# One loop for turns 1 to 9 of the experts, with the overflow part and the residual rows moved ahead of it

## The reference, cut to what matters

```python
for e in range(N_EXPERTS):                       # 32 experts, EXPERT_FF = 512
    h = jax.nn.silu(t @ w_gate[e]) * (t @ w_up[e])
    out = out + combine[:, e:e + 1] * (h @ w_down[e])
```

## Time and profile before

| | |
|---|---|
| three executions | 1076.65, 1077.33, 1078.59 us, median 1077.33 |
| profiled execution | span 1076.0 us, first to last instruction; its time outside the span isn't listed, the median is 1.3 us more |
| busy share of the span | PE 76%, PEld 61%, DVE 29%, ACT 18%, POOL 1% |
| read from memory | 437.84 MB, 408 GB/s over the span |
| chain that ended last | DMA 53%, PE 40%, issue 4%, DVE 2% |
| mean granted TensorE clock | 0.892 |

### The profile page before, as it was taken

The page is one execution under the profiler, slowest core; times in us unless marked ns, Lnnn a source line. Parts: engine busy times, 40 slices in busy tenths (PEclk is TensorE's granted clock), DMA queues, the critical chain, the costliest instruction groups (busy, mean ns, idle before and its releaser), DMA issues.

```text
span 1076.0 us, 30244 instructions
## 1 busy us (share of the span) xinstructions
PE 820.6 (76%) x13956; PEld 653.4 (61%) x13957; DVE 315.3 (29%) x782; ACT 192.6 (18%) x360; POOL 5.4 (1%) x26
## 2 busy tenths in 40 slices
PE   9999989673767667666899999896556767666685
PEld 9778757452654545555599977664354545555463
DVE  5764522211111111111277744221101111111112
ACT  6764211000000000000254331010000000000002
POOL 1000000000000000000000000000000000000000
PEclk9999999987887888888999999998879888888889
DMA  9987999999999999999998599999999999999995
GB/s 375 427 332 282 422 427 427 429 441 425 433 427 434 433 432 431 433 433 421 418 428 336 219 396 424 426 427 429 444 425 428 432 432 433 429 435 433 433 420 242
DMA packets 24948, 439.94 MB, mean 409 GB/s; under 512 B 2992, under 2 KB 3504, under 8 KB 8240
## 3 DMA queue, kind: packets, MB, share of 16 engines
q1 hardware_dynamic: 23904, 437.58, 95.9%
q10 hardware_dynamic: 976, 1.33, 0.4%
HBM read 437.84 MB, written 1.05 MB: 408 GB/s over the span
## 4 chain that ended last, share of the span: by engine, by line
DMA 53%; PE 40%; issue 4%; DVE 2%; SPq 1%; ACT 1%; DVEq 0%; ACTq 0%
DMA ring<-in_expert_weights 50%; PE psum L1579 12%; PE psum L1375 6%; PE psum L1588 6%; PE psum L1448 4%; PE psum L1596 3%; PE psum L1608 3%; PE psum L1427 2%; DMA ring<-in_even_w_in 2%; DMA m<-in_gmlp_w_s 1%; PE psum L1602 1%; PE psum L1700 1%; DVE ring_halves L875 0%; PE psum L1347 0%; PE psum L1334 0%
## 5 line engine op out<-in xcount | busy, mean ns | idle before, releaser
L1579 PE MATMUL psum<-ring,m 128*32 128x128 f32 x7936 | 304.1, 322 | 221.5 <-DMA ring<-in_expert_weights 187.2
L1579 PEld LDWEIGHTS psum<-ring,m 128*32 128x32 f32 x7936 | 280.7, 132 | 252.5 <-issue 177.9
L1236 DVE TENSOR_TENSOR m<-psum,m 128x128 f32<-128x128 f32 x64 | 18.7, 292 | 549.3 <-ACT m L769 532.4
L1588 PE MATMUL psum<-ring,m 128*32 128x256 f32 x1984 | 123.3, 387 | 5.2 <-DMA ring<-in_expert_weights 3.9
L769 ACT ACTIVATE m<-psum 128x128 f32<-128x128 f32 x60 | 16.7, 278 | 497.1 <-PE psum L1579 497.1
L1375 PE MATMUL psum<-scr_halves,ring_halves 128*128 128x256 f32 x736 | 99.1, 284 | 0.2 <-ACT ring_halves L603 0.2
L1588 PEld LDWEIGHTS psum<-ring,m 128*32 128x32 f32 x1984 | 66.1, 113 | 52.9 <-issue 12.1
L1375 PEld LDWEIGHTS psum<-scr_halves,ring_halves 128*128 128x128 f32 x736 | 94.3, 193 | 0.5 <-ACT ring_halves L603 0.5
L1596 PE MATMUL psum<-m 32*128 32x256 f32 x1024 | 81.1, 420 | 10.6 <-issue 8.5
L1608 PE MATMUL psum<-x,m 128*32 128x256 f32 x1024 | 72.7, 402 | 1.4 <-issue 0.8
L1596 PEld LDWEIGHTS psum<-m 32*128 32x128 f32 x1024 | 50.2, 195 | 29.6 <-issue 23.6
(11 more groups left out here) (196 smaller groups left out, 522.5 us busy)
## 6 DMA issues: line engine op xcount, KB each, us to landing
ring<-in_expert_weights SPq DMA_DIRECT2D x36, 6144.0 KB, 33.7
ring<-in_expert_weights SPq DMA_DIRECT2D x76, 2048.0 KB, 21.9
ring<-in_odd_w_in SPq DMA_DIRECT2D x5, 2048.0 KB, 26.0
ring<-in_even_w_in SPq DMA_DIRECT2D x3, 2048.0 KB, 22.2
ring<-in_even_w_out SPq DMA_DIRECT2D x2, 2048.0 KB, 31.4
spare<-in_expert_weights SPq DMA_DIRECT2D x2, 2048.0 KB, 24.7
ring<-in_last_down SPq DMA_DIRECT2D x8, 512.0 KB, 32.1
ring<-in_odd_w_out SPq DMA_DIRECT2D x2, 2048.0 KB, 28.9
```

Source lines behind the costliest of these rows:

```text
L1579: last = pe.matmul(GU[CAP * part:CAP * (part + 1), lo:lo + FP], block_of(k), w_of(k)[:, FP * part:FP * (part + 1)], start=k == 0, stop=k = ...
L1588: last = pe.matmul(YB[CAP * part:CAP * (part + 1), 0:DP], h[:, CAP * f:CAP * (f + 1)], w[:, f, DP * part:DP * (part + 1)], start=f == 0, s ...
```

## The change

- TensorE, ScalarE, VectorE: turn 0 is written out, then come the residual rows (TensorE) and the overflow part, then one loop over turns 1 to 9. `PAUSE`, the expert after which the overflow part stands, goes from 14 to 2.
- SyncE: `overflow` comes after experts 4 and 5 have been issued and ahead of expert 6. The transfers themselves, their sizes and what they wait for stay.
- A whole expert's DMA now counts on `landed` of its gate slot; two `sem_inc` on SyncE raise those of its up and down slots at the issue. TensorE waits for gate's first, so it doesn't use the others early. All later experts use the same three waits.

```diff
-MIDDLE = 5
-PAUSE = MIDDLE * TRI - 1
+PAUSE = TRI - 1
...
+def landed_count(n):
+    return sum(z <= n and place(z) == place(n) for z in COUNTED)
...
-                sp.dma_start(ring[:, SLOT * 3 * at:SLOT * 3 * (at + 1)], expert_weights_in[l, e]).then_inc(whole_landed[at], 16)
+                sp.dma_start(ring[:, SLOT * 3 * at:SLOT * 3 * (at + 1)], expert_weights_in[l, e]).then_inc(landed[3 * at], 16)
+
+                sp.sem_inc(landed[3 * at + 1], 16)
+                sp.sem_inc(landed[3 * at + 2], 16)
...
-                for e in range(EARLY + 2, FINE):
+                for e in range(EARLY + 2, 2 * TRI):
+                    second(l, e)
+                overflow(l)
+                for e in range(2 * TRI, FINE):
                     second(l, e)
...
-                turns(l, ROLLED + 1, MIDDLE + 1)
-                overflow(l)
-                turns(l, MIDDLE + 1, TURNS)
+                turns(l, ROLLED + 1, TURNS)
...
-                for start, stop in ((0, MIDDLE), (MIDDLE, TURNS)):
-                    with act.Fori(start, stop) as b:
-                        for i in range(TRI):
-                            expert(l, b * TRI + i)
-                    if start == 0:
-                        more_experts(l)
+                for e in range(TRI):
+                    expert(l, e)
+                more_experts(l)
+                with act.Fori(1, TURNS) as b:
+                    for i in range(TRI):
+                        expert(l, b * TRI + i)
...
-                for start, stop in ((1, MIDDLE), (MIDDLE, TURNS)):
-                    with dve.Fori(start, stop) as b:
-                        for i in range(TRI):
-                            expert(l, b, i)
-                    if start == 1:
-                        more_experts(l)
+                more_experts(l)
+                with dve.Fori(1, TURNS) as b:
+                    for i in range(TRI):
+                        expert(l, b, i)
...
-            def whole_expert(l, T, i):
-                n = entry(l, FINE + i)
-
-                def wait_weights(mat):
-                    if mat == 0:
-                        pe.wait_ge(whole_landed[place(n) // 3], (T + (whole_count(l, FINE + i) - ROLLED)) * 16)
+                    pe.wait_ge(landed[place(n + mat)], (T + (landed_count(n + mat) - 1)) * 16)
...
-                with pe.Fori(1, ROLLED) as T:
-                    for i in range(TRI):
-                        apart_expert(l, T, i)
-                with pe.Fori(ROLLED, MIDDLE) as T:
-                    for i in range(TRI):
-                        whole_expert(l, T, i)
                 for t in range(TT):
                     put_x(t)
                 more_experts(l)
-                with pe.Fori(MIDDLE, TURNS) as T:
+                with pe.Fori(1, TURNS) as T:
                     for i in range(TRI):
-                        whole_expert(l, T, i)
+                        later_expert(l, T, i)
```

More of the change, by code:

```diff
@@ L76, in third @@
     return place(L_MOE[l] + 3 * i) // 3
-def is_whole(e):
-    return FINE <= e < NE - 2
-SINGLE = [z for z in SPLIT if z not in (L_EVEN, L_EVEN + 1, L_ODD)]
+COUNTED = [z for z in SPLIT if z not in (L_EVEN, L_EVEN + 1, L_ODD)]
 for layer in range(2):
-    for expert in range(FINE):
+    for expert in range(NE):
         if expert != EARLY:
[L87 to L99, removed]
+            COUNTED += [entry(layer, expert) + mat for mat in range(3 - (expert == NE - 1))]
+COUNTED.append(L_GAIN)
+def landed_count(n):
+    return sum(z <= n and place(z) == place(n) for z in COUNTED)
 def pieces(n):
@@ L245, in trunk @@
         landed = [sem(f"landed{i}") for i in range(RING)]
-        whole_landed = [sem(f"whole_landed{i}") for i in range(RING // 3)]
         gate_used, out_half = sem("gate_used"), sem("out_half")
@@ L349, in wait_landed @@
         def wait_landed(eng, n):
-            eng.wait_ge(landed[place(n)], 16 * single_count(n))
+            eng.wait_ge(landed[place(n)], 16 * landed_count(n))
         @contextmanager
@@ L1656, in early_expert, with later_expert @@
                 expert(l, EARLY, EARLY, wait_weights, lambda mat: lambda k: halves[mat][k // HK][:, k % HK, :], spare)
-            def apart_expert(l, T, i):
+            def later_expert(l, T, i):
                 n = entry(l, TRI + i)
                 def wait_weights(mat):
-                    pe.wait_ge(landed[place(n + mat)], (T + (single_count(n + mat) - 1)) * 16)
-                expert(l, T * TRI + i, i, wait_weights, lambda mat: lambda k: wide(n + mat)[:, k, :], tall(n + 2))
-            def whole_expert(l, T, i):
-                n = entry(l, FINE + i)
-                def wait_weights(mat):
-                    if mat == 0:
-                        pe.wait_ge(whole_landed[place(n) // 3], (T + (whole_count(l, FINE + i) - ROLLED)) * 16)
+                    pe.wait_ge(landed[place(n + mat)], (T + (landed_count(n + mat) - 1)) * 16)
                 expert(l, T * TRI + i, i, wait_weights, lambda mat: lambda k: wide(n + mat)[:, k, :], tall(n + 2))
```

## The result

The changed kernel takes 1086.55 us (median of 6, 1083.67 to 1087.56) against 1076.61 (6 runs): ratio 1.0088, 95% interval 1.0078 to 1.0099, 9.9 us slower. The forecast was 1084.1 in a range of 1076.5 to 1091.5. The profiled execution took 1086.27 us with a span of 1084.5, 8.5 more than before.

The account below looks back on a forecast made before the run. DMA bytes bound the MoE stages; TensorE costs time only by letting the queue run dry. 7.5 us lost behind expert 2 less 0.7 us of instruction bytes gives +6.8 on 1077.33: 1084.1 us, range 1076.5 to 1091.5.

Parts of the forecast that it names:

- Place and mechanism: Behind expert 2, TensorE frees expert 3's matrices late, so expert 6's are issued late and the DMA queue runs dry: 7.5 us.
- The terms carried over from expert 14: Standstills and product times measured behind expert 14, applied at expert 3: 10.8 us over both layers, taken as 7.5.
- The first standstill: TensorE's wait between residual rows and the next expert's first matmul, 3.85 and 4.20 us behind expert 14.
- the full second standstill: TensorE's further wait inside expert 3's products, 3.57 us behind expert 14 in layer 0; kept whole, both layers lose 10.8 us.
- the gate term: Expert 6's gate matrix lands late because expert 3's gate is done late: 4.5 us in layer 0, 1.9 in layer 1.
- 3.7 us of rows and then the standstill: Between experts 2 and 3 on TensorE, 3.72 us of residual rows, followed by the whole 3.85 us wait in layer 0.
- What is removed: Two of TensorE's loop body copies per layer go, some 18 instruction blocks, 0.30 MB less on the DMA engines: 0.7 us gained.
- The hidden case: Rival: everything behind expert 2 fits the margins of 4.7 and 6.7 us, nothing is lost: 1076.6 us, chance 0.21.
- The early block end: Rival: a fetch stops TensorE early in expert 3's gate, 7 to 9 us per layer: 1090.6 to 1095.6 us, chance 0.15.
- The loop fetched anew: Rival: the single loop's instructions are fetched again every turn, 1.5 MB, +3.4 us on top: 1087.5 us, chance 0.03.
- SyncE, ScalarE, VectorE and the semaphores: Other engines' reading and branching at the new place, plus extra waits and increments per expert: hidden, costing nothing.

Follow-up runs that it names:

- the run behind turn 1: Changed kernel with residual rows and overflow part moved from behind expert 2 to behind expert 5, on all engines: 1076.32 us, ratio 0.9992 to the kernel before.
- the rows late: Changed kernel with the residual rows moved behind the loop, ahead of the last two experts, overflow part still behind expert 2: 1084.43 us, ratio 1.0063.
- behind turn 4: Changed kernel's loops and three waits per expert, but rows and overflow part at the old place behind expert 14, two loops: 1076.00 us, ratio 0.9994.
- the short body: Changed kernel with TensorE's skipped overflow body cut to a single wait, the branch and the other engines unchanged: 1076.49 us, ratio 0.9996.

## Why the prediction was right, point by point

**Place and mechanism: shown.** The queue ran dry between expert 5's last matrix and expert 6's first, in both layers, because TensorE came late to expert 3's gate. The runs with idle products lose time at the same place with no branch; the run behind turn 1 takes it away with a longer standstill.

**The terms carried over from expert 14.** The first standstill was 3.52 and 3.22 us (3.85 and 4.20 there). Gate was done 7.2 and 8.2 us after the residual rows ended, where I carried over 7.3. The landings behind were 6.5 and 4.0 us late; the sum with the full second standstill had 6.7 and 4.1. I cut 10.8 us to 7.5 because a dry queue should serve a fetch at once. In layer 0 there was indeed no second standstill. But expert 2 ended at 145.2 us instead of 143.3, 1.1 us closer to expert 5's last landing, and the gate matrix took 8.7 us to land in the empty queue instead of 7.6. These two made the gate term 6.5 us instead of 4.5. So it is partly luck that the full sum of 10.8 came so near to what was measured. It has a slip as well: by its own numbers the down matrix of layer 1 would have been 3.2 us late (701.2 against 698.0), so 9.9 us and not 10.8. Counted to expert 6's down matrix, the two places lose 9.65 us instead of 7.5. This is the term that was mis-sized, and most of the 3 us that the forecast lacks.

**"3.7 us of rows and then the standstill" failed as a sum.** It gave about the right total because both had stood in this order behind expert 14 too. Taken apart they overlap: the rows cost 2.2 and 1.3 us of TensorE's time beside the branch, the branch without rows 5.0 and 5.6.

**The clock was not in my sum as a term.** Gate and up took 6.34 us behind the standstill in layer 0 (granted clock 0.50 from 152 to 157 us), 3.63 us where no standstill stood ahead of them. Not every standstill had this behind it: behind the first of layer 1, 3.22 us long, 52 products took 1.72 us at 1.00. It was carried over unnamed, since layer 0 had the same slow products behind expert 14.

**What is removed.** I expected some 18 blocks fewer and found 58 - 40 = 18. Their bytes were put at 0.7 us, and the gain is larger than that. From expert 6's down matrix to the last landing of a layer, the kernels with one loop over turns 1 to 9 need 364.6 to 366.1 us, those with two or three loops (before, its variant without the part, behind turn 1, behind turn 4) 366.8 to 367.7. The rows aren't what makes the difference: with the rows late they stand inside this stretch, at 364.9 and 366.0. In the profiled pair that is 2.9 and 2.2 us. In the medians it shows where nothing else costs: without the overflow part the one loop is at 0.9976 and the three loops at 1.0000. One body less per layer, with a second loop left, gains nothing (0.9992 and 0.9994, with 1 inside both intervals). Where the gain comes from beyond the bytes stays open. The prediction put the end of a layer at nothing ("The last transfers of a layer are issued as before"), but in the profiled pair TensorE was 3.2 us later there in layer 0, which took back more than that layer had gained.

**The hidden case** asked for a standstill of no more than 1.0 us in layer 0. It is what the short body shows. **The early block end** came true in layer 1 in a mild form: a second standstill inside gate, 52 products in, of 2.65 us, not 6.4. **The loop fetched anew** did not happen: 40 blocks in the whole kernel.

**SyncE, ScalarE, VectorE and the semaphores** were costed at nothing; two runs of their own (TensorE without the part, the part behind turn 4) agree, within 0.1 to 0.2%.

**What stays open.** That the standstill is a fetch is argued from its dependence on the unused body and from the block that moves in each of them, not seen. No variant with the overflow part in it beats the kernel before beyond its interval; those behind turn 1 and turn 4 are equal to it. A body short enough to be jumped cheaply that still does the work was not tried.

## What to carry to other kernels

In a stage that is bound by DMA, the price of a stall on TensorE is not its length but its length less the margin of the next transfer that waits for it: the landing time in the trace less the landing time in an empty queue. That landing time isn't one number (7.6 to 9.1 us here), and neither is the moment at which the engine reaches the place, so leave some us of room. Look for the place where the fewest transfers are under way (here the expert whose weights lie outside the ring) and for the end of a layer, where nothing is left to hide TensorE's work behind, and put stalls anywhere else. In these runs a branch over an unused body was such a stall, longer with the full body than with half of it, and the products behind it ran at half clock for some us in part of the cases.

## What the runs showed of the hardware

A branch over a body of 210 matmul records and their weight loads held TensorE for 5.0 and 5.6 us with nothing queued ahead of it. Work queued ahead of the branch hides part of it: with 3.65 us of work the standstill was 3.5 and 3.2 us, with 5.4 us 2.7 and 1.5. I had expected the two to add. Behind the same 3.65 us of work, a body of 82 records gave no standstill at the branch but 1.8 and 2.7 us some 50 to 90 products on, and a single wait none at the branch. What these two cost with nothing queued ahead of them was not measured.

The Trainium skill (Runtime: NRT & Kernel Launch, Instruction fetch mechanics) has the taken branch as a fetch stall, and the runs agree. It has the crossing of a block boundary as mostly hidden. If the later standstills are such crossings, as argued above, they were not hidden with the DMA queues full of weights: 1.8 to 2.7 us in the run with half a body and 4.55 us behind turn 1.
